# Splitting the output products by heads, moving router work between them, and joining an expert's last extra pass with its own pass

## The reference

```python
for l in range(2):
    h = rms_norm(x, attn_norm_w[l])
    proj = h @ w_in[l]
    y_a = windowed_gqa_sink(...)      # 6 heads of 64
    y_b = ssd_mixer(...)              # 6 heads of 64, both directions, ends in rms_norm over 384
    y_c = diff_attention(...)         # 4 heads of 64, ends in rms_norm per head
    x = x + concatenate([y_a, y_b, y_c]) @ w_out[l]          # 1024 x 1024
    h = rms_norm(x, ffn_norm_w[l])
    # router: 4 groups top-1, 8 experts of the group top-2, so 2 of 32 experts per token
    # every expert: (silu(h @ w_gate) * (h @ w_up)) @ w_down, 1024 -> 512 -> 1024
    x = x + hierarchical_moe(h, ...)
return rms_norm(x, final_norm_w)
```

## Time and profile before

| | before |
|---|---|
| median of three runs | 1186.97 us (1186.21 to 1187.02) |
| profiled execution: time, span | 1185.0 us, 1183.3 us |
| mean granted TensorE clock | 0.906 |
| PE busy | 923.9 us, 78% of the span |
| DVE, ACT, POOL busy | 354.0, 202.8, 8.1 us |
| weights' queue (q1) | 434.26 MB, 88.0% of the span of 16 engines |
| PE instructions seen | 11,004 matmuls, 11,004 loads |

### The profile page before, as it was taken

How to read it: one execution, slowest core, us unless ns; L and a number is a source line. 1 busy time by engine, 2 the same in 40 slices (tenths; PEclk the granted TensorE clock), 3 DMA queues, 4 the chain that set the end, 5 groups by cost and what they waited for, 6 DMA issues and landing times.

```text
span 1183.3 us, 26463 instructions
## 1 busy us (share of the span) xinstructions
PE 923.9 (78%) x11004; PEld 587.3 (50%) x11004; DVE 354.0 (30%) x1165; ACT 202.8 (17%) x600; POOL 8.1 (1%) x24
## 2 busy tenths in 40 slices
PE   7999889667678786986699988996666666765954
PEld 6877745333344443553388777453333333433532
DVE  4666343111112232231166645321111111111213
ACT  2275211000001010110124652110000000000001
POOL 2000000000000000000000000000000000000000
PEclk9999989887889998998899999898888888888977
DMA  9853489999999999999996326899999999999995
GB/s 340 319 223 143 151 337 428 429 429 430 429 428 428 429 429 428 412 427 431 405 399 257 124 99 252 353 429 428 430 431 427 431 430 428 431 429 428 428 427 208
DMA packets 50633, 436.17 MB, mean 369 GB/s; under 512 B 9408, under 2 KB 13760, under 8 KB 24640
## 3 DMA queue, kind: packets, MB, share of 16 engines
q1 hardware_dynamic: 50496, 434.26, 88.0%
HBM read 433.20 MB, written 1.05 MB: 367 GB/s over the span
## 4 chain that ended last, share of the span: by engine, by line
PE 46%; DMA 39%; DVE 4%; issue 4%; SPq 2%; DVEq 2%; ACT 1%; ACTq 0%
DMA ring<-in_w_up 38%; PE ps L623 13%; PE ps L711 8%; PE ps L639 5%; PE ps L855 5%; PE ps L648 3%; PE ps L591 3%; PE ps L727 2%; PE ps L611 2%; SPq L462 1%; PE ps L716 1%; DMA ring<-in_w_in 1%; SPq L464 1%; PE ps L824 1%; PE ps L774 1%
## 5 line engine op out<-in xcount | busy, mean ns | idle before, releaser
L623 PE MATMUL ps<-ring,xg 128*32 128x256 f32 x4352 | 314.2, 452 | 173.9 <-DMA ring<-in_w_up 168.6
L623 PEld LDWEIGHTS ps<-ring,xg 128*32 128x32 f32 x4352 | 170.0, 129 | 301.4 <-issue 239.9
L1204 DVE SCALAR_TENSOR_TENSOR th<-th,ps 128x128 f32<-128x128 f32 x72 | 20.7, 287 | 588.1 <-ACT th L977 588.1
L639 PE MATMUL ps<-ring,actT 128*32 128x256 f32 x2304 | 139.2, 382 | 14.1 <-issue 13.2
L977 ACT ACTIVATE th<-ps 128x128 f32<-128x128 f32 x72 | 20.0, 277 | 510.2 <-PE ps L623 474.2
L639 PEld LDWEIGHTS ps<-ring,actT 128*32 128x32 f32 x2304 | 69.0, 109 | 75.3 <-DVE actT L1208 22.6
L591 PE MATMUL ps<-xh,Pb 128*32 128x256 f32 x1152 | 79.5, 394 | 23.4 <-issue 19.4
L711 PE MATMUL ps<-hT,ring 128*128 128x256 f32 x416 | 93.5, 382 | 1.0 <-ACT hT L1014 0.8
L711 PEld LDWEIGHTS ps<-hT,ring 128*128 128x128 f32 x416 | 77.8, 190 | 15.0 <-issue 4.4
L648 PE MATMUL ps<-ysb,PwT 32*128 32x256 f32 x992 | 71.6, 403 | 0.0
L981 ACT ACTIVATE ysb<-ps 128x256 f32<-128x256 f32 x64 | 24.5, 383 | 223.9 <-PE ps L639 223.9
(11 more groups left out here) (259 smaller groups left out, 681.5 us busy)
## 6 DMA issues: line engine op xcount, KB each, us to landing
ring<-in_w_down SPq DMA_DIRECT2D x62, 2048.0 KB, 40.4
ring<-in_w_gate SPq DMA_DIRECT2D x60, 2048.0 KB, 45.2
ring<-in_w_up SPq DMA_DIRECT2D x60, 2048.0 KB, 46.9
ring<-in_w_in SPq DMA_DIRECT2D x6, 2048.0 KB, 15.5
ring<-in_w_out SPq DMA_DIRECT2D x4, 2048.0 KB, 18.6
ring<-in_w_gate SPq DMA_DIRECT2D x8, 1024.0 KB, 29.3
ring<-in_w_up SPq DMA_DIRECT2D x8, 1024.0 KB, 31.3
ring<-in_w_in SPq DMA_DIRECT2D x6, 1024.0 KB, 16.0
```

Source lines behind the costliest of these rows:

```text
L623: last = mm(b_gate[j * SLOTS:(j + 1) * SLOTS, 0:2 * GQ], tokens[:, k, :], ring[:, low:high + 1:high - low, o:o + GQ], start=(k == 0), stop ...
L639: last = mm(b_y[j * SLOTS:(j + 1) * SLOTS, 0:DQ], actT[:, c * SLOTS:(c + 1) * SLOTS], ring[:, slot, o:o + DQ], start=(c == 0), stop=(c == ...
```

## The change

It has six parts.

1. `outA` has only the three blocks of GQA; the three of SSD are a new step `outC`. So outA.0 no longer waits for `yn`, and the second piece of w_out is waited for only at outC.0. outC.3 stands between cn and outB.0.
2. The squares of the SSD output are first added on DVE (two new steps `ya`, 128x256 each), so that `sS` is two products and not six.
3. `fT.j` waits only for its own `xc2.j` and stands between the outB steps; the logits are cut into quarters `lk.0` to `lk.3` that stand between the transposes. fT.0 to .2 are copied out by DVE, fT.3 by ACT (before: 1 and 3 by DVE, 0 and 2 by ACT).
4. ORDER is a new list, also for the front of the mixer.
5. DVE makes `route` behind the preparation of expert 0's tokens, not ahead of it.
6. V's `hidden` writes b_places, not b_gate. For the experts 2 to 30 the extra block no longer goes back to the expert's own block. It runs the combine of the expert before, then the loop only for all extra passes but one (jumped over when there is one), then one joined sequence with the last extra pass and the expert's own pass, and from there jumps to the next expert. The extra blocks of all experts stand one behind the other as before.

```diff
-                    elif kind in ("outA", "outB"):
+                    elif kind in ("outA", "outC", "outB"):
                         if s == ("outA", 0):
-                            w_half = [piece(len(W_IN_PIECES)), piece(len(W_IN_PIECES) + 1)]
+                            w_half = [piece(len(W_IN_PIECES)), None]
                             pe.wait_ge(done["act"], nth(li, "act", ("oa", 0), ("oa", 1), ("oa", 2)))
+                        elif s == ("outC", 0):
+                            w_half[1] = piece(len(W_IN_PIECES) + 1)
                             pe.wait_ge(done["dve"], nth(li, "dve", ("yn",)))
...
                     elif kind == "sS":
-                        pe.wait_ge(done["act"], nth(li, "act", *(("yq", c) for c in range(S_IN // P))))
-                        for t in range(TT):
-                            for c in range(S_IN // P):
-                                last = mm(bank[:, t:t + 1], zT[:, c, t * P:(t + 1) * P], ones[:, 0:1],
-                                          start=(c == 0), stop=(c == S_IN // P - 1))
+                        pe.wait_ge(done["dve"], nth(li, "dve", ("ya", S_IN // P - 1)))
+                        for t in range(TT):
+                            last = mm(bank[:, t:t + 1], zT[:, 0, t * P:(t + 1) * P], ones[:, 0:1], start=True, stop=True)
...
                     elif kind == "fT":
-                        if s[1] == 0:
-                            pe.wait_ge(done["dve"], nth(li, "dve", ("xc2", NQ - 1)))
+                        pe.wait_ge(done["dve"], nth(li, "dve", ("xc2", s[1])))
...
             def hidden(S, tokens, li, e):
+                to = b_places[:, 0:2 * GQ] if S is V else b_gate[:, 0:2 * GQ]
...
+                    own = 2 <= e < NE - 1
+                    if own:
+                        pe.wait_ge(M["y_copied"], n - 1)
+                        pe.wait_ge(M["places_copied"], n - 1)
+                        combine(M, PwT[(e - 1) % 2], ysb)
...
+                    if own:
+                        with pe.If(more_e > 1):
+                            whole(more_e - 1)
+                    else:
+                        whole(more_e)
+                    if not own:
+                        pe.br(f"pe_expert_{n}")
+                        continue
+
+                    i = prev + more_e
+                    gather(V, Pb[(e + 1) % 2])
+                    places(V, Pw[(e + 1) % 2])
+                    hidden(V, xg[(e + 1) % 2], li, e)
+                    hidden(M, xg[e % 2], li, e)
+                    down(V, li, e)
+                    gather(M, Pb[(e + 1) % 2])
+                    combine(V, PwTx, ysbx)
+                    down(M, li, e)
+                    places(M, Pw[(e + 1) % 2])
+                    pe.br_lt(extra_passes(pe, e + 1), 1, on_true=f"pe_expert_{n + 1}", on_false=f"pe_extra_{n + 1}")
```

More of the change, by code:

```diff
@@ L101 @@
 ORDER = """
[L102 to L109, removed]
+    sq xT.0 xT.1 xT.2 xT.3 rs par xbc.1 xbc.3 conv.1 conv.3 xbc.0 dc.1 conv.0 silu.0 xbc.4 xbc.2 conv.2 conv.4 silu.1
+    silu.2 aq.2 dc.0 dt silu.3 dta ak aq.0 lam xs.0 cum silu.4 sc.0 sc.1 cumT nm.0 aS.0 cB z.0 cb.0 nm.1 pT.0 rows.0
+    aq.1 seg.0.0 zs.0 seg.0.1 seg.1.0 seg.1.1 row.0.0 v row.0.1 row.1.1 xs.1 row.1.0 aS.1 sc.2 rows.1 sc.3 nm.2 cb.1
+    ck.0 nm.3 y.0 seg.2.0 z.2 row.2.0 seg.2.1 seg.3.0 yq.0 pT.1 row.2.1 seg.3.1 aS.2 row.3.0 row.3.1 sc.4 seg.4.0 z.1
+    rows.2 nm.4 zs.1 seg.4.1 y.1 yq.1 ck.1 zs.2 ya.1 seg.5.0 row.4.1 row.4.0 seg.5.1 cq.0 pT.2 row.5.1 sc.5 oa.0 row.5.0
+    nm.5 pT.3 cq.1 yq.2 y.2 cS.0 oa.1 pT.4 sc.6 ya.2 sc.7 sS cS.1 pT.5 sc.8 nm.6 yn oa.2 sc.9 sc.10 pT.6 nm.7 outA.0
+    outC.0 pT.7 sc.11 outA.1 nm.8 outC.1 sc.12 sc.13 pT.8 nm.9 outA.2 od.0 pT.9 outC.2 od.1 oS.0 oS.1 outA.3 cn outC.3
+    outB.0 outB.1 xc2.0 sa.0 xc2.1 fT.0 outB.2 sa.1 xc2.2 fT.1 outB.3 xc2.3 fT.2 lk.0 lk.1 sa.2 fT.3 sd lk.2 lk.3 rs2 lg
+    seed wt cnt xn2 rank ov route
 """
@@ L112 @@
 ON_PE = {"xT", "rs", "xbc", "dc", "cq", "aq", "ak", "cum", "xs", "cB", "cumT", "rows", "aS", "cS", "y", "v", "z", "pT", "ck", "oa", "od",
-         "sS", "yn", "oS", "cn", "outA", "outB", "fT", "lg", "seed", "cnt", "rank", "ov"}
-ON_DVE = {"xc2", "wt", "cnt", "sq", "xbc", "cq", "aq", "ak", "ck", "par", "lam", "dt", "dta", "conv", "silu", "cum", "cb", "row", "sc", "nm",
-          "z", "zs", "y", "sS", "yn", "oS", "cn", "sd", "rs2", "lg", "route", "rank", "ov"}
+         "sS", "yn", "oS", "cn", "outA", "outC", "outB", "fT", "lk", "seed", "cnt", "rank", "ov"}
+ON_DVE = {"ya", "xc2", "wt", "cnt", "sq", "xbc", "cq", "aq", "ak", "ck", "par", "lam", "dt", "dta", "conv", "silu", "cum", "cb", "row", "sc", "nm",
+          "z", "zs", "y", "sS", "yn", "oS", "cn", "sd", "rs2", "lg", "rank", "ov"}
 ON_ACT = {"sq", "rs", "par", "lam", "dta", "cumT", "silu", "seg", "sc", "v", "zs", "yq", "pT", "dc", "oa", "od",
           "xT", "xs", "cb", "sa", "xn2", "route"}
+FT_ON_ACT = (3,)
 def shared(step):
@@ L128, in on @@
     if shared(step):
-        return (step[1] % 2 == 0) == (engine == "act")
+        return (step[1] in FT_ON_ACT) == (engine == "act")
     if engine == "dve" and step == ("oS", 0):
@@ L144, in piece_of @@
     kind = step[0]
-    if kind in ("outA", "outB"):
+    if kind in ("outA", "outC", "outB"):
         return len(W_IN_PIECES) + (kind == "outB")
@@ L152 @@
 HT_USERS = [step for step in COUNT["pe"] if piece_of(step) in range(len(W_IN_PIECES))]
[L153 removed]
+LATE_FREED_BY = [("y", S_H // 2 - 1), ("outB", NQ - 1), ("lk", NQ - 1)]
 def freed_when(li, part, n):
@@ L215, in tenants @@
         return [("oS", 1)] * (1 - step[1])
+    if step[0] == "lk":
+        return [("lg",)] * (step[1] == 0)
     return [step]
@@ L233 @@
     for _t in tenants(_s):
-        if _s[0] in ("outA", "outB"):
+        if _s[0] in ("outA", "outC", "outB"):
             _b = _s[1]
@@ L240 @@
         BANK[_t] = _b
-        if _b in _held_by and _s[0] != "outB":
+        if _b in _held_by and _s[0] not in ("outC", "outB"):
             HELD.setdefault(_s, []).append(_held_by[_b])
@@ L853, in _ @@
                         for t in range(TT):
-                            for c in range(2 * REP) if kind == "outA" else range(2 * REP, MC):
+                            for c in range(*{"outA": (0, REP), "outC": (REP, 2 * REP), "outB": (2 * REP, MC)}[kind]):
                                 last = mm(bank[:, t * DQ:(t + 1) * DQ], mixT[:, c, t * P:(t + 1) * P],
@@ new lines, in _ @@
+                    places(V, Pw[(e + 1) % 2])
+                    pe.wait_ge(V["places_copied"], i)
+                    pe.wait_ge(V["xg_ready"], i)
+                    hidden(V, xg[(e + 1) % 2], li, e)
+                    pe.wait_ge(M["xg_ready"], n)
+                    hidden(M, xg[e % 2], li, e)
+                    pe.wait_ge(V["actT_ready"], i)
+                    down(V, li, e)
+                    pe.wait_ge(M["prep_ready"], 2 * n + 1)
+                    gather(M, Pb[(e + 1) % 2])
```

94 lines of the change are left out of this document (51 added, 43 removed).

## The result

The changed kernel takes 1212.57 us (median of four runs, 1209.07 to 1216.26) against 1186.59 us: 26 us more, a ratio of 1.0222 with a 95% interval of 1.019 to 1.0254. The forecast was 1203, with 1194 to 1214 as the range of its likeliest case: the direction and the place were right, the size 9.6 us short. The profiled execution of after has a span of 1207.3 us against 1183.3, so 24.0 us of the difference can be read in it (for after it is the fastest of the four runs, 1209.07 us).

What follows compares the result with a forecast made beforehand. Bound: mixers on PE plus the experts' bytes, with no PE slack at layer 0's expert 22. Sum: 1187.0 - 5.0 (mixers) - 0.4 (route) + 22 (code waits) = 1203.6, said as 1203; likeliest range 1194 to 1214, overall 1179 to 1214.

Steps and rivals of the forecast that it cites:

- likeliest case: Whole kernel: mixers gain, waits for code in layer 0's experts cost more; 1203 us, range 1194 to 1214, chance 0.64.
- What bounds the kernel: Mixers on PE plus the experts' bytes; PE has no slack at layer 0's expert 22, where 0.8 us are lost.
- One packet ahead, 5.9 us each: PE's instruction fetch: entering a packet of about 256 instructions requests only the next, usable 5.9 us later.
- rival B: PE has more than one packet ahead, so skips cost nothing and only far jumps miss: 1180.8 us, chance 0.22.
- The list of waits: PE's waits for code at skips, packet borders and missed jumps in layer 0's experts 14 to 22: 41 us together.
- +22 for the chain: Layer 0's experts 14 to 22: +25.1 us at expert 22's release, less 3 for faster later fetches.
- I took 3 us off: Layer 0's experts: fetches with an idle DMA queue are faster, 3.73 us for one jump, so -3 us.
- The mixers, -5.0: Parts 1 to 5 shorten each layer's mixer on PE by 2.5 us, with 1.8 and 3.2 as ends.
- the route operations: Layer 1, DVE: four route operations ahead of the token transpose cause some of expert 0's 1.47 us hidden wait; -0.4 us.
- the experts' transfers start again at the hidden of expert 0: End of each mixer: weight transfers resume at expert 0's hidden product, so the mixers' whole gain of 5.0 us counts.
- cnt's wait: PE's idle time ahead of cnt in the mixer: 2.4 us in place of 1.98.
- The joined pass itself: Experts with extra passes: idle times of 1.60 and 0.58 us are covered, -2.2 us each if instructions came at once.

Runs made afterwards that it cites:

- the run with the distance alone: Kernel before, with 533 never-run instructions behind every extra block of experts 2 to 30, so blocks lie as far apart as in the changed kernel: 1220.93 us, ratio 1.029.
- the run with the far loops: Changed kernel with the loops over further extra passes moved out of the extra blocks to the end of the program: 1195.15 us, ratio 1.0075.

## Why the prediction was right, and where its size failed

- **What bounds the kernel**: right. Of the 30.8 us by which expert 22's release got later, 28.9 stand at the end of layer 0's experts; in the run with the distance alone it is 33.7 of 36.4 us, and there PE's work is that of before. Of layer 1's single pass nothing did.
- **One packet ahead, 5.9 us each**: right. A packet's border behind a jump was passed 5.5 to 5.9 us after the landing or the border before it. The Trainium skill's rule ("Runtime: NRT & Kernel Launch", "Instruction fetch mechanics") holds with the 5.96, 5.92, 6.74 and 6.03 us of the jumps here. What it says of the size of PE's buffer did not help these jumps: rival B, at 1181, would have needed it, and fell with a profile in which the skips of 269 instructions took up to 5.9 us.
- **The list of waits**: forecast and measured, in us, as "issue" idle of PE: block 14 skip 3.3, measured 2.23; 15: 1.5, measured 1.72; 16: skip and border 3.3 + 3.8, measured 2.32 + 1.34, behind an entry of 6.37; 17: 5.1, measured 4.51; 18: 4.8, measured 5.09; 19: 3.3, measured 3.23; 20: 5.2 + 3.9, measured 5.74 + 2.72. Two small ones of the forecast, 1.3 in block 14 and 1.0 in block 22, aren't there. The measured ones add up to 35 us where I had 41.
- **The term that was too small**: +22 for the chain, measured +28.9 for layer 0's experts. Against the kernel before, the end of each block on PE, and at last the release of 22, moved by these steps:

| | forecast | measured |
|---|---|---|
| start of block 14's way in | 0 | +0.7 |
| 14 and 15 | +2.9 | +3.0 |
| 16 | +9.7 | +10.7 |
| 17 | +2.9 | +3.0 |
| 18 | +2.6 | +3.8 |
| 19 | +1.1 | +1.6 |
| 20 and 21 | +9.1 | +11.8 |
| 22, to its release | -3.2 | -3.7 |
| sum | +25.1 | +30.8 |

I had the slower clock behind each standstill in the range and not in the sum: a combine of 2.09 for 1.15, a gather of 1.94 for 1.07, places of 0.69 for 0.44, and hidden pairs of 7.65 to 10.4 for 7.1 us. In the blocks 16 to 20 this is nearly 14 us of slower products. Not all of it counts: what is slow ahead of a border shortens the wait at the border by as much (the skip of block 14 waited 2.23 us for the 3.3 of the forecast, and its combine took 0.94 longer). It costs in full only behind the last border, as in block 20, where the 40 matmuls of hidden took 4.14 us for 2.3. Second, I took 3 us off because fetches were to be faster with an idle queue. The two jumps made while the queue stood still in part took 6.74 and 6.03 us, and between the release and the end of the layer's experts only 1.9 us went. The 3.73 us on which I had leaned were those of a queue that is idle for good at the end.
- **The mixers, -5.0**: the sum is right (5.2) by luck. I had 2.5 us a layer; between sS and the first hidden product it was 4.1 in layer 0 and 5.0 in layer 1, so the size was too small, and the 4.1 did not reach the end. Of layer 1's 5.2, 0.4 are the route operations (1.47 to 1.06 us ahead of hidden, as forecast) and 1.7 come from outA.3, which in the profile of before ran in 7.11 us there against 5.43 in layer 0, at a granted clock of 0.50 from 710 to 712 us. In all traces here layer 1's mixer takes 145.9 to 147.7 us in the old order and 142.4 to 143.3 in the new. The step that failed is "the experts' transfers start again at the hidden of expert 0, so the whole of it counts": I looked at the queue of PE and of the ring, and passed by SP's own, which in layer 0 has the parameter loads between the mixer and that chunk.
- **cnt's wait** I had growing from 1.98 to 2.4; it is 0.68. seed takes 4.99 us in place of 3.70 (the stretch from 140 to 150 us has a clock of 0.83), so more of the logit chain lies beside it.
- **The joined pass itself** does what it is for: 1.60 and 0.58 ahead of V's down and combine are gone from the joined sequences, and the run with the far loops puts its worth at 2.8 to 3.3 us a pass. What its length costs is more.

## What to carry to other kernels

Code that is reached by a jump has a place, and where an engine has no slack it costs like data: count the instructions between where the engine is and where it goes, and don't put a rarely used loop in the middle of the block that is used. Before a gain on one engine is booked, follow it through the order of the queue that has to pass it on, small loads included; and try a small load on an idle engine's queue before moving it about on a busy one.
